# Hybrid mixer on one core: gating spread over the next group, keys two pairs a slot, query rows by DMA

## What is computed

```python
p = h @ w_in
hc, bc, cc, gc, q, k, v, ga = jnp.split(p, _split_points(), axis=-1)
u = cc * hc
conv_y = sum(conv_w[i] * u_pad[:, i:i + L] for i in range(CONV_WIDTH))
ya = _rmsnorm(bc * conv_y, g_conv) * jax.nn.silu(gc)
...
z = jnp.einsum('bqhd,bkhd->bhqk', q, k).astype(jnp.float32) * (HEAD_DIM ** -0.5)
log_keep = jnp.where(mask, jax.nn.log_sigmoid(-z), 0.0)
after = lax.cumsum(log_keep, axis=3, reverse=True) - log_keep
a = jnp.where(mask, jnp.exp(jax.nn.log_sigmoid(z) + after), 0.0)
return jnp.einsum('bqhk,bkhd->bqhd', a.astype(v.dtype), v)
...
yb = _rmsnorm(o, g_attn) * jax.nn.silu(ga)
m = jnp.concatenate([ya, yb], axis=-1) @ w_out
```

## Time and profile before

| | |
|---|---|
| Time, median of 3 runs (all) | 924.96 us (923.16 to 925.27) |
| The profiled execution | 924.35 us, span 922.6 us, granted clock 0.975 |
| TensorE matmul busy | 845.6 us, 92% |
| VectorE busy | 522.2 us, 57% |
| ScalarE busy | 337.5 us, 37% |
| GpSimd busy | 366.2 us, 40% |
| DMA | 189.14 MB, mean 205 GB/s |

### The profile page before, as it was taken

The page is one execution under the profiler, slowest core; times in us unless marked ns, Lnnn a source line. Parts: engine busy times, 40 slices in busy tenths (PEclk is TensorE's granted clock), DMA queues, the critical chain, the costliest instruction groups (busy, mean ns, idle before and its releaser), DMA issues.

```text
span 922.6 us, 15549 instructions
## 1 busy us (share of the span) xinstructions
PE 845.6 (92%) x4281; PEld 496.5 (54%) x4281; DVE 522.2 (57%) x739; ACT 337.5 (37%) x649; POOL 366.2 (40%) x186
## 2 busy tenths in 40 slices
PE   0899988999999889999998899999988999999996
PEld 0456644555676455565764555658545556434442
DVE  2543498885434578844346788443658883232435
ACT  6311156752202457512025475120346651021112
POOL 0006456661074466600744675017447750100000
PEclk9989999999999899999999999999989999999998
DMA  9986645778377847764778577647875776574101
GB/s 323 332 263 212 217 141 152 235 231 251 92 229 255 272 139 230 242 190 133 235 240 280 167 226 238 199 123 252 259 259 160 225 250 239 199 229 137 71 23 48
DMA packets 128052, 189.14 MB, mean 205 GB/s; under 512 B 9680, under 2 KB 50685, under 8 KB 127952
## 3 DMA queue, kind: packets, MB, share of 16 engines
q1 hardware_dynamic: 96752, 172.27, 57.6%
q10 hardware_dynamic: 31200, 15.73, 6.1%
HBM read 179.49 MB, written 8.49 MB: 204 GB/s over the span
## 4 chain that ended last, share of the span: by engine, by line
PE 63%; SPq 12%; issue 9%; DVE 7%; DMA 3%; POOL 3%; ACT 1%; DVEq 0%; POOLq 0%; ACTq 0%
PE ps L1104 59%; SPq L342 5%; SPq L350 5%; PE ps L1260 3%; POOL prod L513 3%; DMA ring<-in_cache_v_dram 2%; DVE ps L984 2%; PE ps L1145 1%; DMA pages<-in_page_table_dram 1%; DVE zc L990 1%; DVE zd L960 1%; SPq L310 1%; DVE xy L788 1%; DVE zc L970 1%; DVE zx L857 0%
## 5 line engine op out<-in xcount | busy, mean ns | idle before, releaser
L513 POOL TENSOR_TENSOR prod<-ring,qb 128x1024 f32<-128x1024 f32 x128 | 306.6, 2403 | 339.3 <-DVE zd L960 150.8
L1104 PE MATMUL ps<-hT,wsl 128*128 128x344 f32 x1344 | 436.4, 467 | 2.3 <-issue 2.3
L1104 PEld LDWEIGHTS ps<-hT,wsl 128*128 128x128 f32 x1344 | 246.6, 194 | 160.8 <-issue 52.7
L960 DVE TENSOR_REDUCE zd<-prod 128x16 f32<-128x1024 f32 x128 | 155.2, 1213 | 41.1 <-POOL prod L513 41.1
L970 DVE TENSOR_SCALAR zc<-ps,bsb 128x512 f32<-128x512 f32 (+3 forms) x96 | 55.0, 613 | 91.4 <-PE ps L1104 91.2
L1104 PE MATMUL ps<-ring,apad 128*8 128x512 f32 x512 | 70.4, 624 | 15.8 <-DMA ring<-in_cache_v_dram 15.7
L547 ACT ACTIVATE av<-ps 128x512 f32<-128x512 f32 (+3 forms) x96 | 46.7, 486 | 94.1 <-PE ps L1260 93.8
L547 ACT ACTIVATE rise<-ps,bsh 128x512 f32<-128x512 f32 (+3 forms) x96 | 55.5, 578 | 65.7 <-DVE zc L970 65.3
L984 DVE TENSOR_TENSOR_SCAN ps<-rise,ps 128x512 f32<-128x512 f32 (+3 forms) x64 | 65.5, 1023 | 22.5 <-ACT ps L547 21.9
L1104 PE MATMUL ps<-hT,xy 128*128 128x512 f32 x160 | 72.3, 596 | 0.0
L1260 PE MATMUL ps<-ident,zc 128*128 128x128 f32 x288 | 49.1, 280 | 21.0 <-DVE zc L990 21.0
(11 more groups left out here) (215 smaller groups left out, 668.6 us busy)
## 6 DMA issues: line engine op xcount, KB each, us to landing
ring<-in_cache_k_dram SPq DMA_DIRECT2D x256, 256.0 KB, 3.0
ring<-in_cache_v_dram SPq DMA_DIRECT2D x256, 256.0 KB, 3.0
wsl<-in_w_in_dram ACTq DMA_DIRECT2D x30, 512.0 KB, 5.4
ring<-in_w_ada_dram SPq DMA_DIRECT2D x6, 2048.0 KB, 11.6
xy<-in_x_prompt_dram SPq DMA_DIRECT2D x2, 2048.0 KB, 10.4
out_dram<-oT SPq DMA_DIRECT2D x8, 512.0 KB, 3.7
ring<-in_x_prompt_dram SPq DMA_DIRECT2D x8, 512.0 KB, 6.2
hT<-in_w_out_dram SPq DMA_DIRECT2D x5, 512.0 KB, 5.0
```

The costliest lines, as they stand in the source:

```text
L513: pool.tensor_tensor(prod[:, t % 2].rearrange("p (j c) -> p j c", j=2), kring[:, t % 4], qb[:, t // 16].unsqueeze(1).to_broadcast([P, 2, H ...
L960: v.tensor_reduce(zd[:, t // 16, :, r:r + 2], prod[:, t % 2].rearrange("p (j h d) -> p h j d", j=2, h=NH), AX_X, ALU.add)\
L1104: return nc.tensor.matmul(out, l, r, start=start, stop=stop, skip_group_check=True)
```

## The change

Seven things change.

- `pairs_at` gives the key pairs of a slot: two in each of slots 0 to 7, then 16 pairs over slots 8 to 31. SyncE, GpSimd and VectorE follow it.
- The gating of group `g - 1` becomes six steps in slots 0 to 5 of group `g`, each behind the reduces of its slot. ScalarE's squares stand in slots 3 and 5. After the last group the six steps follow each other.
- Query rows: TensorE gathers the eight rows once, they go to DRAM (`q_rows`), and SyncE loads each over all partitions (`load_q`). `seq_q` and `spread_q` go.
- Value quads are requested two slots ahead of their use; the slots of `quad_of` move a little; the first quad of the group's second sequence is requested at the end of the group's program.
- `decode_clamp` goes; ScalarE's `decode_logs` takes Abs, Relu, Exp and Ln. It stands in slot 9 instead of 17, `cumulate(0)` in 12 instead of 19, `decode_log_weights(0)` in 14 instead of 20.
- The copies of key rows and of the first half of the output move from VectorE to ScalarE (`key_rows` itself from slots 8 and 9 to 6 and 7).
- SiLU steps move to slots 15 to 30; group 0's gate steps move to slots 1 to 6 (VectorE: 0 and 5).

```diff
-MS = 7
-M_QB0, M_KN0, M_KN1, M_KNS, M_QB1, M_CUM0, M_CUM1 = range(MS)
+MS = 5
+M_KN0, M_KN1, M_KNS, M_CUM0, M_CUM1 = range(MS)
...
+def pairs_at(slot):
+
+    if slot < 8:
+        return (2 * slot, 2 * slot + 1)
+    late = [s for s in range(8, SLOTS) if s % 2 or s % 6 == 2]
+    return (16 + late.index(slot),) if slot in late else ()
...
-    for parity, slots in ((1, (1, 3, 5, 7, 8, 10, 12, 14)), (0, (22, 24, 26, 28, 30, 31, 32, 33))):
+    for parity, slots in ((1, (1, 3, 6, 8, 10, 12, 14, 16)), (0, (20, 22, 24, 26, 28, 30, 32, 33))):
...
+            def load_q(g, k):
+
+                sp_e.dma_start(qb[:, k, :], q_rows[bass.ds(2 * g + k, 1), :].to_broadcast([P, HALF])).then_inc(q_full[k], 16)
...
+                if not first:
+                    sp_e.wait_ge(prod_ready, 32 * g - 16)
+                    load_q(g, 0)
...
-                    numbers = pair_numbers(2 * g + t // 16, 2 * (t % 16))
-                    if not (first and t < 4):
-                        sp_e.wait_ge(prod_ready, 32 * g + t - 3)
-                    load_pair(kring[:, t % 4], cache_k, numbers, k_full[t % 4])
-                    if first and t == 5:
+                    for p in pairs_at(t):
+                        numbers = pair_numbers(2 * g + p // 16, 2 * (p % 16))
+                        if not (first and p < 4):
+                            sp_e.wait_ge(prod_ready, 32 * g + p - 3)
+                        load_pair(kring[:, p % 4], cache_k, numbers, k_full[p % 4])
+                    if first and t == 1:
+                        sp_e.wait_ge(qs_copied, 2)
+                        sp_e.dma_start(q_rows, qsP[0:NB, :]).then_inc(q_out, 16)
+                        sp_e.wait_ge(q_out, 16)
+                        load_q(g, 0)
+                        load_q(g, 1)
                         load_ada(7, ada_v[5])
-                    if first and t == 22:
+                    if not first and t == 3:
+                        sp_e.wait_ge(prod_ready, 32 * g)
+                        load_q(g, 1)
+                    if first and t == 18:
                         sp_e.wait_ge(ada_ps, 6)
-                    load_quad(g, first, t)
-                    if t == 12:
+                    load_quad(g, first, t + 2)
...
-                load_quad(g, first, SLOTS)
-                load_quad(g, first, SLOTS + 1)
+                for rr in range(2):
+                    load_v(2 * g + 1, rr, 16 * g + 7)
...
-                    if t % 16 == 0:
-                        pool.wait_ge(ms_free, MS * g + (M_QB1 if t else M_QB0) + 1)
-                    pool.wait_ge(k_full[t % 4], 32 * (8 * g + t // 4 + 1))
-                    if not (first and t < 2):
-                        pool.wait_ge(red_done, 32 * g + t - 1)
-                    pool.tensor_tensor(
-                        prod[:, t % 2].rearrange("p (j c) -> p j c", j=2), kring[:, t % 4],
-                        qb[:, t // 16].unsqueeze(1).to_broadcast([P, 2, HALF]), ALU.mult).then_inc(prod_ready, 1)
-                    if t == 17:
+                    for p in pairs_at(t):
+                        if p % 16 == 0:
+                            pool.wait_ge(q_full[p // 16], 16 * g + 16)
+                        pool.wait_ge(k_full[p % 4], 32 * (8 * g + p // 4 + 1))
+                        if not (first and p < 2):
+                            pool.wait_ge(red_done, 32 * g + p - 1)
+                        pool.tensor_tensor(
+                            prod[:, p % 2].rearrange("p (j c) -> p j c", j=2), kring[:, p % 4],
+                            qb[:, p // 16].unsqueeze(1).to_broadcast([P, 2, HALF]), ALU.mult).then_inc(prod_ready, 1)
+                    if t == 8:
                         decode_scores(g, 0, first)
-                        silu_min(g, 0)
-                    if t == 18:
+                    if t == 10:
                         decode_softplus(g, 0)
-                    if t in (19, 25):
-                        silu_mul(g, t // 25)
-                    if t == 23:
-                        silu_min(g, 1)
+                    if t in (18, 28):
+                        silu_min(g, t // 28)
+                    if t in (22, 30):
+                        silu_mul(g, t // 30)
...
+            def decode_logs(g, k):
+                act.wait_ge(d_zb, 2 * g + k + 1)
+                run(zx[:, :], zb[:, :], ACT.Abs, d_abs)
+                run(spd[:, :], zb[:, :], ACT.Relu, d_rise)
+                act.wait_ge(d_abs, 2 * g + k + 1)
+                run(zx[:, :], zx[:, :], ACT.Exp, d_exp, scale=-1.0)
                 act.wait_ge(d_exp, 2 * g + k + 1)
                 run(zx[:, :], zx[:, :], ACT.Ln, d_ln, bias=1.0)
...
+            def out_copy(g):
+
+                act.wait_ge(pv_done, NU * g + 8)
+                act.wait_ge(kout, 16 * (g + 1))
+                run(oT[:, 0:QC], ps[:, OB, :], ACT.Copy, o_free)
+
+            def squares(g, half_):
+
+                if half_ == 0:
+                    act.wait_ge(o_free, g + 1)
+                    act.wait_ge(ob_ready, g + 1)
+                    run(tmp[:, 0:SEQ], oT[:, :], ACT.Square, sq_done)
+                else:
+                    act.wait_ge(bconv_ready, g + 1)
+                    run(gab[:, 0:SEQ], hcb[:, 0:SEQ], ACT.Square, sq_done)
...
+                        if t in (3, 5) and not first:
+                            squares(g - 1, t // 5)
+                    if t == 19:
+                        out_copy(g)
+                    if t >= 8 and t < SLOTS and u % 2 == 1:
                         evac(g, first, last, 9 + u // 2)
-                    if first and t in (4, 10):
-                        gate_strips(t // 10)
-                    if t in (14, 15, 16):
-                        silu_step(g, 0, t - 14)
-                    if t in (20, 21, 22):
-                        silu_step(g, 1, t - 20)
-                    if t in (18, 24):
-                        silu_end(g, int(t == 24))
-                    if t == 17:
-                        decode_ln(g, 0)
-                    if t == 20:
+                    if first and t in (1, 5):
+                        gate_strips(t // 5)
+                    if t == 9:
+                        key_rows_copy(g, 2, first)
+                    if t in (15, 25):
+                        silu_step(g, t // 25, 0)
+                    if t in (17, 27):
+                        silu_step(g, t // 27, 1)
+                        silu_step(g, t // 27, 2)
+                    if t in (21, 29):
+                        silu_end(g, t // 29)
+                    if t == 9:
+                        decode_logs(g, 0)
+                    if t == 19:
...
-                def decode_clamp(k):
-
-                    v.wait_ge(d_zb, 2 * g + k + 1)
-                    v.tensor_scalar(spd[:, :], zb[:, :], CLAMP, 0.0, ALU.subtract, ALU.max).then_inc(d_rise, 1)
-                    v.tensor_scalar(zx[:, :], zb[:, :], CLAMP, None, ALU.min).then_inc(d_zx, 1)
...
+                    if t == 14:
+                        decode_log_weights(0)
+                    if t == 18 and not first:
+                        own_heads(1)
+                    if t == 20 and not first:
+                        own_heads_copy(1)
                     if u >= 0 and u % 2 == 0:
                         clamp(g, u, first)
                         clamp(g, u + 1, first)
                     if t > 0:
-                        reduce_pair(g, t - 1)
-                    if t == 18:
-                        out_copy(g, 0)
-                    if first and t in (6, 12):
-                        gates(t // 12)
-                    if t in (8, 9):
-                        v.wait_ge(ms_full, MS * g + M_KN0 + t - 8 + 1)
-                        v.tensor_copy(kN[:, 4 * (t - 8):4 * (t - 7), :],
-                                      ps[:, MB, :].rearrange("p (t c) -> p t c", t=4)).then_inc(ms_free, 1)
-                    if t == 10:
-                        v.wait_ge(ms_full, MS * g + M_KNS + 1)
-                        v.tensor_copy(kS[:, bass.ds(g * P, P)], ps[0:NB, MB, 0:P]).then_inc(ms_free, 1)
-                    if t == 11:
-                        seq_q(g, 1)
-                    if t == 13:
-                        seq_q_copy(g, 1)
-                    if t == 16 and not first:
-                        own_heads(1)
-                    if t == 17:
-                        if not first:
-                            own_heads_copy(1)
-                        decode_clamp(0)
-                    if t == 20:
-                        decode_log_weights(0)
+                        for p in pairs_at(t - 1):
+                            reduce_pair(g, p)
+                    if not first:
+                        gating(g - 1, t)
+                    if first and t in (0, 5):
+                        gates(t // 5)
...
-                out_copy(g, 1)
...
+            def gating(g, step):
+
+                if step == 0:
+                    out_copy(g)
+                if step == 1:
+                    v.wait_ge(silu_done, 2 * g + 2)
```

(32 more changed lines are left out.)

116 lines of the change are left out of this document (40 added, 76 removed).

## The result

The changed kernel takes 874.43 us (median of 4 runs, 872.5 to 876.23); the kernel before took 925.12 us beside it (4 runs, 923.16 to 925.35). The ratio is 0.9447, 95% interval 0.9413 to 0.948: faster by 5.5%. The prediction was 875 us, range 867 to 895. The profiled execution took 872.5 us, with a span of 870.7 us.

A forecast was written before the change was run, and what follows sets the result against it. TensorE was taken to bound the groups. Idle time 33.5, clock 11.8 and TensorE's work 6.0 sum to 51.3 us; from 924.35 that gives 873.0, 873.6 as median, plus 1.5 for short waits: 875 us, range 867 to 895.

The forecast's parts named there:

- TensorE bounds the groups: In all four groups, only TensorE's losses can be won: idle 33.5 us, clock 11.8, its own work 6.0.
- Earlier start: Group's start: SyncE reaches query row and keys at -14 us, first pair landed -9, products -4, reduces +3.
- SyncE: Page requests at 2.27 us a pair: slot 10's quad by +48 us; value waits inside groups, 14.0 us, gone.
- GpSimd and VectorE in slots 0 to 7: Gating beside products: gating ends +36 us, product 15 +47, first log weights +52, wanted +53; hidden by 1 us.
- SiLU at nothing: SiLU in odd slots: nothing taken for TensorE; upper bound 1.54 us at four places, 6 us.
- Reduces moved out of slots 8 to 31: VectorE's 24 reduces become 16, 10 us a group; only slack for log weight waits, 21.0 us counted as gone.
- TensorE's own work and the clock: Eight query row spreads go, 6.0 us; six 10 us stretches behind waits that go lose 11.8 us of clock.
- Group 0: After the second gate step VectorE needs 17.3 us, TensorE 14.7: new wait 2.6 us, estimated 0 to 6.
- Rival 1: Pages late again at slots 8 to 16, 6 us in each of 3 groups: 893 us; chance 0.12.
- Rival 2: VectorE and GpSimd serial in slots 0 to 7, slot 9 waits about 4 us: 895 us, partly 884; chance 0.17.
- Rival 3: ScalarE holds slot 5's projection until gating step 2; each us beyond +37 costs three; chance 0.03.
- Rival 4: Log weight waits stay in slots 13 to 20, 17 us of the gain not had: 891 us; chance 0.08.

The follow-up runs named there:

- a_hold: Changed kernel with the next group's query row and keys held until TensorE has finished its chunk of slot 0: 916.18 us.
- b_q: Kernel before with one part of the change, query rows by DMA alone: 907.78 us, ratio 0.9828.
- a_sp: Changed kernel with SyncE loading the page numbers of key pairs 4 to 7 twice in groups 1 to 3: 882.05 us.
- a_end: Changed kernel with the gating whole at the end of each group again: 888.69 us.
- b_logs: Kernel before with decode_clamp alone taken off VectorE, ScalarE making Abs and Relu in slot 17: 908.21 us, ratio 0.9807.
- a_silu: Changed kernel with the SiLU steps back in slots 14 to 25: 877.51 us.
- a_one: Changed kernel with one key pair a slot, and the first sequence's decode steps and value quads in their slots of before: 879.75 us.
- a_g0: Changed kernel with group 0's second gate step back in slots 9 to 12: 876.05 us.
- b_v: Kernel before with value quads requested two slots sooner alone: 925.16 us, ratio 1.003.
- b_qv: Kernel before with both query rows by DMA and values two slots sooner: 927.41 us, ratio 1.0034.
- b_ql: Kernel before with two parts, query rows by DMA and decode_clamp on ScalarE: 893.18 us, ratio 0.9699.

## Why the prediction was right, step by step

- **TensorE bounds the groups; only its idle time, its clock and its own work can be won.** Right. Idle time 32.0 us won where 33.5 was predicted; clock and TensorE's work together 21.3 where 11.8 + 6.0 = 17.8 was, so this term was 3.5 too small. The 1.5 us allowed for short waits are just what the idle time fell short by. Outside the groups the program grew by 1.4 us, which no term had. 924.35 - 53.3 + 1.4 = 872.5 is the profiled execution; the other three runs are 0.7 to 3.7 us longer, so the median lies 1.9 above it, where the prediction took 0.6. That 875 and 874.43 agree within 1 us is in part luck: the 3.5 us by which one term was too small are made up by 1.4 and 1.3 us that weren't in the sum.
- **Earlier start.** First key request at -13.0 (predicted -14), landed at -9.0 (-9), products 0 and 1 ended at -4.3 (-4), first reduce +2.4 (+3). a_hold shows that this is what most of the gain rests on, b_q that it moves the value waits by itself.
- **SyncE.** The quads of slots 10, 12, 14 and 16 were requested by +45.9, +53.3, +61.2 and +71.3; predicted +48, +55, +62 and +72. No value wait in a group. The price of 2.27 us a pair carried this. a_sp shows how thin the cover is: 4.5 us more of SyncE's time a group cost 2.6 as a mean.
- **GpSimd and VectorE in slots 0 to 7.** The blocking is as predicted in kind: L971 took 2.52 us and L986 2.53, where the same two (L933 and L947) took 1.27 and 1.28 before. Four long instructions and the scan of step 2 took 13.0 us a group as a mean (12.97 from the rows below), though the last group's have no product beside them:

```profile
L990 DVE TENSOR_TENSOR ssb<-ssb,tmp 128x1024 f32<-128x1024 f32 x4 | 15.1, 3786 | 0.0
L974 DVE TENSOR_TENSOR_SCAN last<-naught,ub 128x2 f32<-128x2 f32 x4 | 10.9, 2718 | 0.0
L986 DVE SCALAR_TENSOR_TENSOR xy<-hcb,par,gcb 128x1024 f32 (+1 forms) x4 | 8.9, 2216 | 0.0
L971 DVE SCALAR_TENSOR_TENSOR xy<-oT,par,gab 128x1024 f32 (+1 forms) x4 | 8.8, 2212 | 0.0
L993 DVE TENSOR_TENSOR ssa<-ssa,gab 128x1024 f32<-128x1024 f32 x4 | 8.2, 2038 | 0.5 <-ACT gab L572 0.5
```

  (VectorE's groups by line in the changed kernel: busy us in all, mean ns.) The gating ended at +34.1 (predicted +36), product 15 at +45.8 (+47), the last reduce at +52.5 (+51), the log weights at +53.2 (+52), wanted at +53.6 (+53): slack 0.4 instead of 1 us. By the Trainium skill, SBUF — State Buffer, section "Who interferes with whom", a VectorE instruction with two SBUF inputs is fully blocked by a GpSimd instruction that reads SBUF and came first. The trace agrees: L990, with both inputs in SBUF, took 4.65 us beside products, and the same instruction of a_end without them 1.22, as these rows show with the scan:

```profile
231.11 0.15 DVE L972 TENSOR_TENSOR_SCAN last<-naught,ub 128x2 f32<-128x2 f32 x1
...
234.13 1.22 DVE L988 TENSOR_TENSOR ssb<-ssb,tmp 128x1024 f32<-128x1024 f32 x1
```

  But the rule alone doesn't give the sign: with four of the five long steps and the scan blocked (L983 met no product and took 1.22), spreading the gating still gains 14 us over a_end.
- **decode_clamp.** Right, and b_logs shows it alone: the 2.66 us wait goes, and only one of 0.28 is new.
- **SiLU at nothing.** Right within 3 us (a_silu). The prediction left open whether the 1.54 us wait was SiLU's; it was not.
- **Reduces moved out of slots 8 to 31.** Right in direction, small: at most 5 us (a_one), most of which is the decode step in slot 20. The waits for log weights were not due to the number of reduces.
- **TensorE's own work and the clock.** TensorE's busy time in the groups fell by 21.3 us. The page's largest group of matmuls is the same work in both kernels, 1344 records of the same shape, and took (before, then after):

```profile
L1104 PE MATMUL ps<-hT,wsl 128*128 128x344 f32 x1344 | 436.4, 467 | 2.3 <-issue 2.3
L1144 PE MATMUL ps<-hT,wsl 128*128 128x344 f32 x1344 | 425.3, 458 | 3.5 <-issue 3.5
```

  That is 11.1 us of clock alone; the transposes (49.1 to 47.3) and value products (70.4 to 69.2) add 3.0. So some 14 us were clock, where 11.8 was forecast. The records of the spreads took 8.2 us in all, the product that came instead takes 1.0: some 7, where 6.0 was forecast. The clock term was too small by the two stretches behind the loop's jump, 410 to 430, at 0.94 and 0.89 before, 1.7 us; the prediction counted only stretches behind waits that go. The jump did stay, but no stretch of 10 us in the groups from 60 on is now below 1.00. Why the clock holds there isn't shown.
- **Group 0.** The new wait is 2.08 us (with three short ones 2.7; predicted 2.6), the group 175.2 us (174 to 178). But the working was wrong in a part, so the agreement is luck: it put VectorE's 5.2 us for the second gate step at the head of the sum, and a_g0 shows a wait of 2.77 us without that step there. What bounds it then is GpSimd's stream of 16 products behind the query row and the first gate step; with 8 products ahead of slot 9 the wait is gone (a_one).
- **Rivals.** Rival 1, late pages: not seen. Rival 2, serial VectorE and GpSimd: the small copies took 0.17 us each, but no product ran beside them (none between 240.93 and 244.58), so that they would lose no turn isn't shown; a scan of two columns (L974) lost one, 3.57 us, and so did L990, whose 4.65 us reach over two products; it stayed hidden by 0.4 us. Rival 3: step 2 ended at +16.4 (I had +17, the limit is +37). Rival 4, waits that only change their name: no log weight wait is left in groups 1 to 3. In b_v and b_qv, between value pages and log weights, just this happened.
- **Where a range was missed.** Group 1 took 165.9 us (166 to 170), TensorE idled 7.85 us in groups instead of about 6, and L990 took 4.65 us where gating instructions were to take 1.2 to 3.6.

What stays open: one part alone gives 17 us (b_q), another 16 (b_logs), together 28 of 51, each against the kernel before beside it (against 924.96, b_ql's is 32). The remaining 19 to 23 us can't be shared out by adding, since taken away singly the spreading gives 14, the sooner values 11, the two pairs with their decode steps 5 and SiLU up to 3, together 33. They hold each other up.

## What to carry to other kernels

Where several engines take work strictly in order, walk each queue for what a moved instruction stands behind: a request that waits for a buffer stops every request behind it, and asking for values sooner cost 20 us while the keys behind it were needed, and gained 11 once they were ahead. Give every queue that only hands out work (SyncE here, 2.27 us a pair) a line in the sum: the one expectation that left it out (a_end) was off by 14 us. Work that blocks another engine for a few us may still be well placed, if it lets that engine start sooner.

## What the runs showed of the hardware

- A VectorE scan of two columns, both inputs in SBUF, took 3.57 us beside GpSimd's products and 0.15 without them (a_end).
- A blocked VectorE instruction may wait for two products in a row: L990 took 4.65 us, where it takes 1.22 without products; it ended 1.1 us behind the second (255.07).
- Products beside such instructions came at 10.49 us for four (2.62 each), without them at 18.92 for eight (2.36 each, a_end), so both engines lose. Over all 128 products of the program the mean is 2470 ns in the changed kernel and 2402 in a_end.
- Loading the page numbers of a pair a second time took SyncE 1.1 us; twelve such loads in the program cost 7.6 us (a_sp): register loads on SyncE aren't free when it has little idle time.
